# A scan stage with its recurrence steps placed elsewhere in each group, and state steps ahead of the inverse

## What is computed

```
u = t_inv @ (v * beta);  w = t_inv @ (k_beta * exp(g))
step:  v_new = u - w @ s;  o = q_dec @ s + (qk masked) @ v_new
       s = s * exp(g_last) + k_end.T @ v_new
```

## Time and profile before

| | us |
|---|---|
| median of three runs | 4424.25 |
| profiled execution | 4422.44 |
| its span, first to last instruction | 4420.6 |
| busy in the span: PE | 3905.9 (88%) |
| VectorE | 2150.2 (49%) |
| GpSimd | 1062.0 (24%) |
| ScalarE | 973.5 (22%) |
| scan, layer one | about 575 to 1133 |
| scan, layer two | about 2747 to 3303 |

### The profile page before, as it was taken

How to read it: one execution, slowest core, us unless ns; L and a number is a source line. 1 busy time by engine, 2 the same in 40 slices (tenths; PEclk the granted TensorE clock), 3 DMA queues, 4 the chain that set the end, 5 groups by cost and what they waited for, 6 DMA issues and landing times. The chain is left out here.

```text
span 4420.6 us, 80619 instructions
## 1 busy us (share of the span) xinstructions
PE 3905.9 (88%) x33780; PEld 3012.8 (68%) x33780; DVE 2150.2 (49%) x4904; ACT 973.5 (22%) x1962; POOL 1062.0 (24%) x1092
## 2 busy tenths in 40 slices
PE   4999968888897999999779998788879799999994
PEld 3444446676556999999744444566664399999994
DVE  3335045665555444444453340556646464454544
ACT  2233134444210000000033331444431100000001
POOL 0036035444210100011040450354533000100003
PEclk9999978888998999999989998898889899999997
DMA  7457353332526888888564752334235368888884
GB/s 268 169 188 252 130 132 73 87 70 63 193 76 229 280 285 290 280 292 284 179 227 153 247 198 65 95 81 93 59 94 203 118 225 289 293 282 282 280 292 171
DMA packets 557878, 836.19 MB, mean 189 GB/s; under 512 B 85864, under 2 KB 403368, under 8 KB 551372
## 3 DMA queue, kind: packets, MB, share of 16 engines
q1 hardware_dynamic: 474476, 720.51, 49.9%
q10 hardware_dynamic: 67840, 71.59, 4.9%
q0 software_dynamic: 15200, 38.94, 3.5%
HBM read 698.83 MB, written 132.10 MB: 188 GB/s over the span
## 5 line engine op out<-in xcount | busy, mean ns | idle before, releaser
L2590 PE MATMUL ffn_hb<-ffn_xT,ffn_w 128*128 128x144 f32 x8192 | 1048.5, 286 | 0.0
L2590 PEld LDWEIGHTS ffn_hb<-ffn_xT,ffn_w 128*128 128x128 f32 x8192 | 1019.6, 190 | 2.3 <-issue 1.0
L521 PE MATMUL front_acc<-late,front_xmT 128*128 128x512 f32 (+2 forms) x2304 | 879.1, 541 | 17.5 <-DVE front_xmT L782 17.5
L521 PEld LDWEIGHTS front_acc<-late,front_xmT 128*128 128x128 f32 x2304 | 438.3, 192 | 444.1 <-issue 417.7
L2598 PE MATMUL ffn_acc<-ffn_hT,ffn_w 128*128 128x144 f32 x4096 | 547.1, 287 | 0.0
L2598 PEld LDWEIGHTS ffn_acc<-ffn_hT,ffn_w 128*128 128x128 f32 x4096 | 518.5, 190 | 6.7 <-issue 6.7
L2633 ACT ACTIVATE ffn_en<-ffn_hb 128x144 f32<-128x144 f32 x256 | 74.5, 291 | 1447.2 <-PE ffn_hb L2590 1447.2
L2513 POOL DMA_INDIRECT ffn_xe<-scratch_xhat,ffn_g_idx x34 | 34.3, 1008 | 1476.7 <-DVEq L2698 1434.5
L2742 DVE TENSOR_TENSOR ffn_hT<-ffn_en,ffn_hb 128x144 f32<-128x144 f32 x256 | 77.8, 304 | 582.5 <-ACT ffn_en L2633 582.1
L2277 PE MATMUL mixer_acc<-late,mixer_oT 128*128 128x512 f32 x576 | 250.7, 593 | 3.0 <-ACT mixer_oT L2243 3.0
L2659 DVE TENSOR_SCALAR_CACHE_REDUCE ffn_junk<-ffn_row,ffn_pair 128x128 f32<-128x128 f32 (+2 forms) x324 | 245.4, 757 | 1.4
(11 more groups left out here) (346 smaller groups left out, 5181.1 us busy)
## 6 DMA issues: line engine op xcount, KB each, us to landing
ffn_w<-in_w_e SPq DMA_DIRECT2D x384, 1024.0 KB, 9.2
x_res<-in_w_mod SPq DMA_DIRECT2D x40, 1024.0 KB, 5.5
x_res<-scratch_proj SPq DMA_DIRECT2D x36, 768.0 KB, 6.0
scratch_proj<-front_out ACTq DMA_DIRECT2D x90, 256.0 KB, 2.2
ffn_row<-scratch_affT SPq DMA_DIRECT2D x36, 576.0 KB, 4.3
late<-in_w_in ACTq DMA_DIRECT2D x8, 2048.0 KB, 12.2
early<-scratch_qkv SPq DMA_DIRECT2D x16, 1024.0 KB, 10.3
scratch_qkv<-x_res SPq DMA_DIRECT2D x18, 768.0 KB, 3.5
```

Of the source, the lines that this page charges most:

```text
L521: mm = pe.matmul(acc[:, U % 2, 0:size], xmT[:, k, t * P:(t + 1) * P], w[:, n % 2, k, 0:size], start=k == 0, stop=k == KD - 1)
L2590: mm = pe.matmul(hb[:, b, i * CAP:(i + 1) * CAP], w[:, r, k, c:c + P], xT[:, s, k, :], start=k == 0, stop=k == KD - 1)
```

## The change

Groups 1 to 4 of each layer, on all engines but GpSimd:

- Recurrence steps: step 0 stays in the front, but PE's `write_state` comes after the `decays`. In groups 2 to 4 steps 1 and 2 lie in the solve, where 2 and 3 lay; the last step (3, or 1 of group 0) moves into the tail: PE reads between `merge_x` and `merge_z` and writes between the first and second pair of `weights` and `values`; VectorE does its part after all `inverse` transposes.
- VectorE does both `gla_state` steps of the second half before `inverse_for_x`, PE issues them one behind the other before its last attention steps.
- Groups 2 to 4: VectorE's `attend(at)` moves from between the two `block_in` pairs to behind `gla_scaled`; PE and ScalarE move `attend(at + 2)` behind `gla_turn` (on PE behind `gla_scores` too).
- Group 1: the second half's GLA steps come one attention step earlier on PE and ScalarE.
- `small` goes between the two `turn_keys`.
- SP's stores and loads stand in another order; `load_v` goes to the end of a pass.

PE, then VectorE (ScalarE's follows PE's, shortened; SP's is told above):

```diff
@@ PE, groups above 0
-                        for i in range(n):
-                            turn_keys(g, i)
+                        turn_keys(g, 0)
+                        small(g)
+                        turn_keys(g, 1)
                         read_state(k, 0)
                         for i in range(n):
                             turn_queries(g, i)
-                        write_state(k, 0)
                         for i in range(n):
                             decays(g, i)
-                        read_state(k, 1)
-                        for m in range(2):
-                            grams(g, m)
-                        write_state(k, 1)
-                        for m in range(2, chunks[g]):
+                        write_state(k, 0)
+                        for m in range(chunks[g]):
                             grams(g, m)
                         attend(at)
@@ PE, group 1, second half
-                        attend(at + 8)
                         gla_gates(g, h)
+                        attend(at + 8)
+                        gla_turn(g, h)
                         attend(at + 9)
-                        gla_turn(g, h)
+                        gla_scores(g, h)
                         attend(at + 10)
-                        gla_scores(g, h)
+                        gla_values(g, h)
                         attend(at + 11)
-                        gla_values(g, h)
-                        attend(at + 12)
                         gla_state(g, h, 0)
-                        attend(at + 13)
                         gla_state(g, h, 1)
-                        attend(at + 14)
+                        for i in range(12, 15):
+                            attend(at + i)
@@ PE, groups above 1
                         attend(at + 1)
-                        read_state(k, 2)
+                        read_state(k, 1)
+                        gla_turn(g, h)
+                        gla_scores(g, h)
                         attend(at + 2)
-                        gla_turn(g, h)
-                        write_state(k, 2)
-                        gla_scores(g, h)
+                        write_state(k, 1)
                         attend(at + 3)
                         gla_values(g, h)
-                        read_state(k, 3)
+                        read_state(k, 2)
...
                         gla_state(g, h, 0)
+                        gla_state(g, h, 1)
                         attend(at + 10)
-                        gla_state(g, h, 1)
                         attend(at + 11)
@@ PE, tail
+                    if g:
+                        read_state(k, chunks[k] - 1)
                     for i in range(n):
                         merge_z(g, i)
-                    for i in range(n):
-                        weights(g, i)
-                        values(g, i)
+                    weights(g, 0)
+                    values(g, 0)
+                    if g:
+                        write_state(k, chunks[k] - 1)
+                        weights(g, 1)
+                        values(g, 1)
@@ VectorE
                         write_state(k, 0)
-                        read_state(k, 1)
-                        for m in range(2):
-                            masked_grams(g, m)
-                        write_state(k, 1)
-                        for m in range(2, chunks[g]):
+                        for m in range(chunks[g]):
                             masked_grams(g, m)
                         block_in(g, (0, 1))
-                        attend(at + (g == 1))
+                        if g == 1:
+                            attend(at + 1)
                         block_in(g, (2, 3))
...
                     if g > 1:
+                        attend(at)
+                        gla_masked(h)
+                        read_state(k, 1)
+                        attend(at + 2)
+                        write_state(k, 1)
                         read_state(k, 2)
-                        attend(at + 2)
-                        write_state(k, 2)
-                        gla_masked(h)
-                        read_state(k, 3)
...
                     if g:
+                        gla_state(h, 0)
+                        gla_state(h, 1)
                         inverse_for_x(g)
-                        gla_state(h, 0)
                         inverse(1, ta_v)
-                        if g > 1:
-                            inverse(2, ta_v)
-                        gla_state(h, 1)
-                        if g == 1:
-                            inverse(2, ta_v)
+                        inverse(2, ta_v)
                         inverse(0, tb_v)
                         inverse(3, tb_v)
+                        read_state(k, chunks[k] - 1)
+                        write_state(k, chunks[k] - 1)
                         attend(at + (13 if g == 1 else 10))
```

More of the change, by code:

```diff
@@ L1141, in _ @@
                         load_next()
+                    if g == GROUPS:
+                        for m in range(4):
+                            store_gdn(k, m)
+                        break
                     if k >= 0:
-                        for m in range(2):
-                            store_gdn(k, m)
-                    if g < GROUPS:
-                        if k >= 0 and g + 1 < GROUPS:
+                        store_gdn(k, 0)
+                        if g + 1 < GROUPS:
                             load_gates(g + 1)
-                        if g + 1 < GROUPS:
-                            load_qk(g + 1)
-                        h = halves[g][0]
-                        if h < 8:
-                            load_gla(h + 1)
-                    if k >= 1:
-                        for m in range(2, 4):
-                            store_gdn(k, m)
-                    if k >= 0 and k + 2 < GROUPS:
-                        load_v(k + 2)
+                    if g + 1 < GROUPS:
+                        load_qk(g + 1)
+                    if k >= 1:
+                        store_gdn(k, 1)
+                    if halves[g][0] < 8:
+                        load_gla(halves[g][0] + 1)
+                    if k >= 1:
+                        store_gdn(k, 2)
+                    for h in halves[g]:
+                        if h != halves[g][0] and h < 8:
+                            load_gla(h + 1)
+                        store_gla(h)
+                    if k >= 0:
+                        store_gdn(k, chunks[k] - 1)
+                        if k + 2 < GROUPS:
+                            load_v(k + 2)
                     if k == 0:
@@ L1163, in _ @@
                                 sp.dma_start(state("new_gla", d, a), SG[half(a), 0, d]).then_inc(s_out, 16)
-                    if g < GROUPS:
-                        for h in halves[g]:
-                            if h != halves[g][0] and h < 8:
-                                load_gla(h + 1)
-                            store_gla(h)
                 sp.wait_ge(s_out, 129)
@@ L1459, in _ @@
                     h = halves[g][0]
-                    small(g)
                     if g == 0:
+                        small(g)
                         turn_keys(g, 0)
@@ L1546, in _ @@
                         gla_state(g, h, 1)
-                        write_state(k, 3)
+                        write_state(k, 2)
                         h = halves[g][1]
@@ L1734, in _ @@
                     else:
-                        for i in range(n):
-                            turned(g, i, 0, kT_p, kT_a)
+                        turned(g, 0, 0, kT_p, kT_a)
+                        small(g)
+                        turned(g, 1, 0, kT_p, kT_a)
                         for i in range(n):
@@ L1750, in _ @@
                         gla_values(h)
-                        for i in range(6, 9):
+                        for i in range(6, 8):
                             attend(at + i)
@@ L1754, in _ @@
                         gla_gates(h)
+                        attend(at + 8)
+                        gla_turned(h)
                         attend(at + 9)
-                        gla_turned(h)
                         attend(at + 10)
-                        attend(at + 11)
                         gla_values(h)
-                        for i in range(12, 15):
+                        for i in range(11, 15):
                             attend(at + i)
```

3 lines of the change are left out of this document (1 added, 2 removed).

## The result

The changed kernel takes 4462.34 us, median of four runs (4454.62 to 4468.59), against 4424.09 us (4423.12 to 4424.47): a ratio of 1.0079, 95% interval 1.0067 to 1.0091. It is slower, and outside the predicted range (4406 to 4437). Its profiled execution took 4454.62 us (span 4452.8, clock 0.940), 32.2 us more than that of before.

A forecast was written before the change was run, and what follows sets the result against it. The prediction took the chain front, solve, VectorE's tail, PE's tail as the bound. Group 2's gain 7.6, group 3's 0.4, group 4's 3.9, less group 1's 13.0, gave -1.1 us: forecast 4423 us, range 4406 to 4437.

The forecast's parts named there:

- the prediction's two terms, 2.2 and 2.0: Front of groups 2 to 4: masked grams end 2.2 us earlier, attention step between block turns (2.0 us) goes; gain 3.9.
- 3.7 for the two state steps: Before the inverse transposes: VectorE does both GLA state steps, the second needing PE again, 0.6 + 1.2 + 0.6 + 1.2.
- 7.6 for group 2: Group 2 gains 3.6 + 0.1 us and about the same in layer two, 7.6 for both.
- Rival B: Groups 2 to 4: solve still decides, PE catches up; 48 us faster, 4375; chance 0.07.
- A's marks: Clock returns before `scores` (2.3 us after `gla_turn`), group 1 loses only 3.5: 13 us better, 4410; chance 0.27.
- Rival D: Solve: VectorE's added 5.4 us stop GpSimd, solve ends at t 74.4; 4426; chance 0.06.
- rival C: Groups 2 to 4: low clock through `scores` and weighing, 3.8 not 1.2; group 1 at 9; 21 us slower, 4443; chance 0.17.
- where 1.2 was taken: Groups 2 to 4, after `gla_turn`: low-clock loss in `scores`, weighing and `gla_scores`, between nothing and 3.8 us.
- First failed step: the queue of groups 2 to 4: PE's later queue, not the solve, sets the inverse: t 76.6 in group 3 against 73.2 before.
- Second failed step: the tail: Unbroken transposes let `weights` start 12.25 us after the inverse's start, gain 5.2; moved `write_state` costs 1.6: net 3.6 a group.
- Third failed step: group 1: Second half's new order: inverse 8.5 us late, tail returns 1.9; loss 6.5, bounds 3.5 and 9.

The follow-up runs named there:

- e5: Changed kernel with group 1's second half as before, and groups 2 to 4's attention step between the turns, scores ahead of gated attention's turn again: 4406.3 us, 0.9943 of before.
- e7: e5 with the second half's two state steps of groups 2 to 4 back between the inverse transposes: 4438.5 us, 1.0020 of before.
- e4: Changed kernel with the second half's two state steps of groups 2 to 4 back between the inverse transposes: 4465.0 us, 1.0088 of before.
- e12: e6 with step 0's state write ahead of the decay matmuls again, both recurrence steps in the front: 4409.0 us, 0.9961 of before.
- e10: e5 with PE's `write_state` of step 0 ahead of the decay matmuls again: 4408.8 us, 0.9957 of before.
- e11: Kernel before with only the scores step of groups 2 to 4 moved behind gated attention's turn and scores: 4439.2 us, 1.0031 of before.
- e6: e5 with the moved last recurrence step put back second in the front, none in the tail: 4430.9 us, 1.0004 of before.
- e9: e5 with group 1's two state steps also ahead of the inverse transposes, its order otherwise old: 4399.8 us, 0.9944 of before.

## Why the prediction was wrong

**Confirmed.** In groups 2 and 3, and in group 4 of layer two, t counted from `small` as there, the front ended at t 29.1 (predicted 29.0) and the solve at 68.8 to 68.9 (69.4); PE idled 5.4 us before the turn (5.4; 7.1 in group 4 of both layers, where its queue ahead of the turn is shorter); `scores` moved behind it; the solve no longer decided: the inverse started 5.1 us or more after it. The front gained 4.2 us (33.3 to 29.1), which is what the prediction's two terms, 2.2 and 2.0, add up to; it wrote 3.9. (Two smaller sums, 3.7 for the two state steps and 7.6 for group 2, are 0.1 and 0.2 too high.) Rival B never appeared, and A's marks (`scores` at 2.3 us, group 1 losing 3.5) neither. Rival D didn't appear in size, but the changed kernel hardly tried it: the 5.4 us of VectorE work that were to be added to the solve did not fall in it (20.04 us busy against 19.97; the solve 39.79 us, and 39.95 in e5 with 21.87). The blocking rule of the Trainium skill (SBUF — State Buffer, "SBUF: two separate sides") does show in the solve, in VectorE's instructions with two SBUF inputs alone, and costs some 2 us a solve in groups 2 to 4 of the kernel before already (last section).

**The clock.** In all six groups the low clock reached through most of `scores` (3.9 to 4.2 us, over 4 in five of them; 4.17 and 4.12 in the rows above), which was the mark set for rival C; the weighing behind it ran at the high clock again (2.12 us). With group 1 at its bound, C would have come to 4443, still 19 us short. The cost is 1.9 us in `scores` and 0.4 in `gla_scores` (1.13 against 0.69), 2.3 us where 1.2 was taken, inside the bounds.

**First failed step: the queue of groups 2 to 4.** The inverse was forecast at t 72.9, 76.6 and 74.6 in groups 2, 3 and 4. It started at 74.0, 75.8 and 76.5 in layer one, at 74.1, 77.7 and 78.5 in layer two. By the forecast's own changes against before (9.9 us over six groups; measured 18.1) that is 8.2 us. About 1.1 us of each is the clock; what is left is mostly group 4, the worst sized, whose second-half gates waited 1.7 and 3.0 us for the GLA load (0.6 and 0.7 before) and came at t 54.6 and 54.9 (50.5 and 49.1 before), so that its gain in layer two didn't come.

**Second failed step: the tail.** The prediction let VectorE's last transposes set `weights`, 12.25 us after the inverse's start, and credited 3.6 us a group. In e5 it was nearly so: 12.6 to 13.3 us. In the changed kernel it was 12.6 to 12.8 in three groups and 13.9 to 14.9 in the other three. Two things delay PE there. Attention steps 10 and 11 stand behind the second state step and hold the merges back: in group 2 until 5.4 us after the inverse's start (rows above), where VectorE had freed them after 4.0 and e5 starts them after 4.0 to 4.2. And PE stops on nothing that the profile shows, 10.0 us in these six tails against 3.4 in e5 (last section); in group 3 of layer one, whose merges start no later than e5's, only these stops (3.2 us) are left. No run parts the two. From the inverse's start to the last `values` the six groups took 25.6 us on average before and 23.4 after: 2.2 credited, not 3.6; 8.4 us over six.

**Third failed step: group 1.** Its inverse was forecast 8.5 us late and was 8.7 and 7.2 us late. But 1.9 us was to come back in its tail, and 2.3 and 3.3 us more were lost there. The three attention steps in the rows above kept the merges until 8.6 and 8.8 us after the inverse's start (9.0 before), so the unbroken transposes brought nothing; and from the merges to the last `values`, with the moved recurrence step and some 2 us of PE's stops between them, it took 17.3 and 17.5 us (14.7 and 14.0 before). Forecast 6.5 each, measured 10.96 and 10.54: 8.5 us together, beyond the bound of 9 each.

These three, 8.2, 8.4 and 8.5, and the 5.9 us outside the eight groups, which the forecast had at nothing and whose cause stays open, make 31.0 of the 31.6 us between forecast and profiled execution. Beside these sizes the sum lacked one thing: it priced the state steps ahead of the inverse and PE's later queue as two terms, though each sets what the other is worth. The runs give the four corners for groups 2 to 4, all with the last step in the tail:

| groups 2 to 4, us | state steps between the transposes | ahead of them |
|---|---|---|
| scores ahead of the turn | 607.5 (e7) | 569.1 (e5) |
| scores behind the turn | 609.7 (e4) | 601.6 (changed) |

The steps ahead are worth 6.4 us a group if PE brings them by the solve's end (in e5 the inverse starts 0.2 to 1.8 us after it), and 1.35 if it is late (5.1 to 9.6 us in the changed kernel). Between the transposes the scores' place costs 0.4 us a group, ahead of them 5.4. So the edit that freed VectorE's 2.0 us in the front took most of the gain of the edit in the tail. The moved recurrence step has such partners too: with the unbroken run of transposes it costs nothing in these groups (e12 to e10), and with the decays first as well it gains 5.4 (e12 to e5). In e7, which has it without that run, they are 10.7 us slower than before, but no run parts it there from e7's other edits.

## What to carry to other kernels

When an edit makes an engine's step wait for the end of another engine's queue, its worth depends on the slack of that queue, so walk the queue with all other edits in it before crediting anything behind it. An attention step that stands ahead of a wait is the filler of that wait: moved behind it, its length shows up twice, once as idle time (8.1 to 8.7 us in e11 against 4.3 to 4.6 before) and once, here at the lower clock, as work ahead of what is late next. Try the parts of such a change in pairs: here the state steps ahead of the inverse were worth 6.4 us a group in one company and 1.35 in another, and the decays ahead of the write gained 5.6 us beside the moved step (e10 to e5) and lost 12.6 without it (e12 to e6).

## What the runs showed of the hardware

PE's unexplained stops in the tails were not expected. Over the changed kernel the waits of TensorE whose cause is "issue", that is nothing that the profile shows, by line (in all, times, longest):

```profile
PE scan_pR L1296 <- issue: 6.3, 5, 1.6
PE scan_pA L1252 <- issue: 5.0, 7, 1.4
```

With those at the other matmuls of the tail it is 14.3 us in eight tails against 0.2 before, 0.4 to 3.2 us each; e9 has 11.4 us. In the changed kernel these tails run at a mean granted clock of 0.72 to 0.90 between merge X and the last `values`, the tails of before at 0.61 to 0.76. But the clock doesn't part the tails that stop from those that don't: six of e12's stop for 19.3 us at 0.60 to 0.80, and two of e9's at 0.90 don't stop; all of e5's, with the changed kernel's instructions in the tails of groups 2 to 4, stop for 4.4 us. In a tail of the changed kernel four or five loads of about 16 KB pass on the DMA queue for instructions, in one of before three or four (267 in the whole run, 4.37 MB). Group 2's tail holds 642 matmuls and 642 weight loads. The Trainium skill (Advanced Engine Details and Errata, "ISA Cache") gives 16 KB as one cache line of 256 instructions; by that, as an estimate, these would be five lines, and the trace, with four or five loads a tail, agrees. Whether PE waits for these loads no run shows, since none took them away; it stays open.

GpSimd's solve answers to one kind of VectorE instruction. First the kernel before, then the changed one, both in group 2: the same GpSimd product beside a VectorE product of two SBUF tiles, and beside a reduction.

```profile
829.69 0.72 DVE L1902 TENSOR_TENSOR scan_sdec<-scan_S,scan_eg 128x512 f32<-128x512 f32 x1
829.94 0.65 POOL L1817 TENSOR_TENSOR scan_prod<-late 128x58 f32<-128x58 f32 x1
```

```profile
837.56 1.34 DVE L1986 TENSOR_REDUCE scan_top<-x_res 128x1 f32<-128x1152 f32 x1
837.81 0.32 POOL L1822 TENSOR_TENSOR scan_prod<-late 128x58 f32<-128x58 f32 x1
```

The 590 of 600 instructions of `substitute` in the kernel before that can be compared with the same instruction in another solve say so throughout: beside a VectorE operation on two SBUF tiles (82 of them) they take 0.19 us longer on average; beside VectorE instructions that read PSUM, reduce or scale, none is over 0.05 us longer. The ten solves take 38.2 to 39.9 us, and without these excesses each takes 37.7.
